# Two layer mixers in another order, with their masks built three heads at a time and 16 chunks' low parts on GpSimd

## The reference

```
proj = h @ w_in                          # 256 x (gate 384, rec 384, z 384, xbc 896, dt 6, uv 512)
rec  = causal_dwconv(rec, 4 taps);  r, i = sigmoid(rec @ w_r + b_r), sigmoid(rec @ w_i + b_i)
a    = exp(-8 r softplus(-lam));    u = sqrt(1 - a*a) * i * rec
ya   = scan(h = a*h + u) * gelu(gate)                        # "recurrent branch", 384 wide
xbc  = silu(causal_dwconv(xbc, 4 taps)); xs, B, C = split(xbc)   # "state-space branch"
dt   = softplus(dt + dt_bias);      ad = dt * -exp(a_log);   cs = cumsum(ad)
yb   = sum_s (C.B)[l,s] * exp(cs[l]-cs[s]) [s<=l] * dt[s] * xs[s] + d_skip * xs   # six heads
yb   = rms_norm(yb * silu(z))
u, v = split(gelu(uv)); v = layer_norm(v); yc = u * (tril(w_s) @ v + b_s)         # "u-v branch"
out  = concat(ya, yb, yc) @ w_out
```

## Time and profile before

| | |
|---|---|
| median of 3 runs | 1672.4 us (1672.17 to 1672.96) |
| profiled execution, its own time | 1670.92 us |
| its span, first to last instruction | 1669.2 us |
| PE busy, share of the span | 94% |
| DVE, ACT, POOL busy | 65%, 48%, 5% |
| mean granted clock of PE | 0.948 of full speed |

### The profile page before, as it was taken

One profiled execution on the slowest core, in us unless ns is written; L12 is line 12 of the kernel. 1 busy time (PEld: TensorE's weight loads), 2 busy tenths in 40 slices (PEclk: granted clock), 3 DMA queues, 4 the chain that ended last, 5 costly groups with the idle time before them and its releaser, 6 DMA issues.

```text
span 1669.2 us, 27509 instructions
## 1 busy us (share of the span) xinstructions
PE 1563.6 (94%) x10201; PEld 1409.1 (84%) x10201; DVE 1083.9 (65%) x1756; ACT 794.6 (48%) x1299; POOL 91.7 (5%) x116
## 2 busy tenths in 40 slices
PE   6999998899999999989799999899888789999999
PEld 5999888789998999979679999698666469989998
DVE  4555686665557655577666555657899966655555
ACT  5333457363335533365644333546476644453332
POOL 0000000000000000010000000103121210000000
PEclk9999998799999999998889999989888779999999
DMA  7555553155555655545135555446111115645552
GB/s 284 189 186 188 187 166 114 61 167 190 187 180 175 230 189 188 181 144 181 38 126 189 187 181 187 134 152 227 64 63 64 38 56 184 194 149 189 186 181 99
DMA packets 71081, 261.88 MB, mean 157 GB/s; under 512 B 8016, under 2 KB 8016, under 8 KB 70736
## 3 DMA queue, kind: packets, MB, share of 16 engines
q1 hardware_dynamic: 69696, 253.79, 46.1%
q10 hardware_dynamic: 1296, 6.85, 1.1%
HBM read 259.56 MB, written 1.05 MB: 156 GB/s over the span
## 4 chain that ended last, share of the span: by engine, by line
PE 77%; DVE 15%; ACT 6%; issue 2%; DMA 1%; POOL 0%; ACTq 0%; DVEq 0%
PE work L437 18%; PE work L439 17%; PE work L438 17%; PE acc L437 7%; PE acc L438 7%; PE acc L439 7%; DVE wlo L432 3%; ACT whi L425 1%; DVE g L1851 1%; DVE rs L1858 1%; DVE sm L1859 1%; DVE xbcc L1099 1%; DVE h L1844 1%; DVE sg L1843 1%; DVE frac L1712 0%
## 5 line engine op out<-in xcount | busy, mean ns | idle before, releaser
L432 DVE TENSOR_TENSOR wlo<-raw,whi 128x1024 fp32r<-128x1024 f32 x480 | 571.5, 1217 | 232.2 <-ACT whi L425 228.6
L437 PE MATMUL work<-xhi,whi 128*128 128x256 f32 x2160 | 616.4, 285 | 7.3 <-DVE wlo L432 5.9
L439 PE MATMUL work<-xhi,wlo 128*128 128x256 f32 x2160 | 613.0, 284 | 0.0
L438 PE MATMUL work<-xlo,whi 128*128 128x256 f32 x2160 | 612.8, 284 | 0.0
L425 ACT ACTIVATE whi<-raw 128x1024 fp32r<-128x1024 f32 x480 | 476.8, 1043 | 28.9 <-PE acc L439 15.9
L437 PEld LDWEIGHTS work<-xhi,whi 128*128 128x128 f32 x2160 | 416.2, 193 | 12.8 <-issue 6.1
L438 PEld LDWEIGHTS work<-xlo,whi 128*128 128x128 f32 x2160 | 416.3, 193 | 4.5
L439 PEld LDWEIGHTS work<-xhi,wlo 128*128 128x128 f32 x2160 | 416.1, 193 | 0.0
L765 ACT ACTIVATE sg<-sg 128x256 f32<-128x256 f32 x100 | 41.9, 419 | 495.9 <-DVE sg L803 495.9
L437 PE MATMUL acc<-whi,hhi 128*128 128x512 f32 x440 | 174.6, 397 | 0.0
L438 PE MATMUL acc<-wlo,hhi 128*128 128x512 f32 x440 | 174.0, 396 | 0.0
(11 more groups left out here) (406 smaller groups left out, 1736.9 us busy)
## 6 DMA issues: line engine op xcount, KB each, us to landing
raw<-stream SPq DMA_DIRECT2D x480, 512.0 KB, 4.2
par<-pm ACTq DMA_DIRECT2D x2, 1644.5 KB, 6.9
pfa<-pf_a ACTq DMA_DIRECT2D x3, 516.0 KB, 3.5
pfb<-pf_b ACTq DMA_DIRECT2D x2, 516.0 KB, 7.9
x<-x_in SPq DMA_DIRECT2D x2, 512.0 KB, 6.3
out<-x SPq DMA_DIRECT2D x2, 512.0 KB, 2.6
par<-pm ACTq DMA_DIRECT2D x1, 820.0 KB, 4.5
pre<-pf_a ACTq DMA_DIRECT2D x1, 4.0 KB, 4.4
```

What stands on the lines that cost most here:

```text
L432: nc.vector.tensor_tensor(chunk(wlo, place, c)[:, cols], chunk(raw, place, c)[:, cols], chunk(whi, place, c)[:, cols].bitcast(F32), ALU.su ...
L437: return [nc.tensor.matmul(o, lhi, rhi, start=start, stop=False), nc.tensor.matmul(o, lhi, rlo, start=False, stop=False), nc.tensor.matmul ...
L438: nc.tensor.matmul(o, lhi, rlo, start=False, stop=False),
L439: nc.tensor.matmul(o, llo, rhi, start=False, stop=stop)]
```

## The change

The order of the mixer's 30 chunks is now: z and dt together in four (`zdt`, 390 columns; the fourth chunk has 48 used columns and only those are split), xbc in seven (B and C first: `XBC_ORDER`), rec in three, gates in three, the padding, u-v in four, `w_out` in eight. PE's program follows, with `cbt` right behind the first rec chunk, the head sums for heads 0 to 2 ahead of the recurrent gates, those of 3 to 5 behind them, all six heads' matmuls behind the gate chunks, u-v behind those, and the mixing `sgu` behind three output chunks. Exponents are kept for three heads together (`dm`, 128x1152), so that ACT does two exponentials and DVE two multiplications (`weights`) instead of six and twelve; dt is multiplied into xs while it is emptied (`xdt`). The low parts of chunks 6 to 21 are made by GpSimd.

```diff
-C_UV, C_REC, C_XBC, C_DT, C_GATE0, C_GATE1, C_Z, C_PAD, C_OUT = 0, 4, 7, 14, 15, 16, 18, 21, 22
-OUT_ORDER = [6, 7, 0, 1, 2, 3, 4, 5]
+C_ZDT, C_XBC, C_REC, C_GATE, C_PAD, C_UV, C_OUT = 0, 4, 11, 14, 17, 18, 22
+ZDT = BW + HEADS
+BY_POOL = range(6, C_OUT)
+XBC_ORDER = [3, 4, 5, 6, 0, 1, 2]
+OUT_ORDER = [0, 1, 2, 3, 4, 5, 6, 7]
+BANKED = (["zdt0", "zdt1"] + [f"xbc{b}" for b in XBC_ORDER] + ["rec0", "cs", "rec1", "rec2", "xtok0", "xtok1", "csb0", "csb1", "csb2"]
+          + [f"lru{b}" for b in range(AB)] + ["csb3", "csb4", "csb5", "gate0", "gate1", "gate2", "uv0", "uv1", "sgu0", "sgu1"]
+          + ["ybt0", "ybt1", "ybt2", "yct0", "yct1"])
+        def split_lo_pool(pool, place, cs):
+            pool.wait_ge(lo_ready, place.count(cs[0] - 1))
+            for c in cs:
+                cols = used(place, c)
+                pool.wait_ge(hi_ready, place.count(c))
+                nc.gpsimd.tensor_tensor(chunk(wlo, place, c)[:, cols], chunk(raw, place, c)[:, cols], chunk(whi, place, c)[:, cols].bitcast(F32),
+                                        ALU.subtract).then_inc(lo_ready, 1)
...
+            for i, b in enumerate(XBC_ORDER):
+                projected(C_XBC + i)
+                emptied(f"xbc{b}", nc.scalar.activation(xbcpad[:, b, 3:], bank(f"xbc{b}", slice(0, S)), ACT.Copy))
+                split_hi(act, place, [C_XBC + i + 6])
+                if i == 5:
+                    activated(range(0, 4))
+            recurrent(0)
+            activated(range(4, 7))
+            recurrent(1)
+            recurrent(2)
+            decays(0)
...
+            def exponents(g):
+                vec.wait(dve, 1)
+                for h in range(3 * g, 3 * g + 3):
+                    job.wait(dve, JOB[f"csb{h}"])
+                    o = dm[:, g, h % 3]
+                    nc.vector.scalar_tensor_tensor(out=o[:, 0:S], in0=bank(f"csb{h}", slice(0, S)), scalar=ncs[:, 0, h:h + 1], in1=maskadd[:, :], op0=ALU.add, op1=ALU.add)
...
+            def weights(g):
+                dexp.wait(dve, g + 1)
+                job.wait(dve, JOB["cbt"])
+                m_ready.inc(nc.vector.tensor_tensor(dm[:, g], dm[:, g], acc[:, 1, g * 512:g * 512 + 384].unsqueeze(1).broadcast_to([P, 3, 384]), ALU.mult))
```

More of the change, by code:

```diff
@@ L885, in release @@
                     m.then_inc(consumed, 1)
-            begin(pe, BANKED, "uv0")
-            done("uv0", tokens("uv0", 0, C_UV, 2 * CW, first=True)[-1])
+            begin(pe, BANKED, "zdt0")
+            done("zdt0", tokens("zdt0", 0, C_ZDT, ZDT, first=True)[-1])
             turn_xn(pe, q, r, 1)
[L890 to L895, removed]
@@ new lines, in mix_pe @@
+            done("cbt", m)
+            begin(pe, BANKED, "cs")
+            ad_ready.wait(pe, 1)
+            tri, ones = upper[:, 0:P], upper[:, P:S]
+            nc.tensor.matmul(bank("cs", slice(0, HEADS)), tri, ad[:, 0, :], start=True, stop=True)
+            nc.tensor.matmul(bank("cs", slice(8, 8 + HEADS)), ones, ad[:, 0, :], start=True, stop=False)
+            done("cs", nc.tensor.matmul(bank("cs", slice(8, 8 + HEADS)), tri, ad[:, 1, :], start=False, stop=True))
+            channels("rec1", C_REC + 1)
@@ new lines, in mix_pe, with sums @@
+            channels("rec2", C_REC + 2)
+            xbc_act.wait(pe, XB)
+            for t in range(T):
+                begin(pe, BANKED, f"xtok{t}")
+                for b in range(AB):
+                    m = nc.tensor.transpose(bank(f"xtok{t}", slice(b * P, (b + 1) * P)), xbcc[:, b, t * P:(t + 1) * P], ident[:, :])
+                done(f"xtok{t}", m)
+            def sums(h):
+                begin(pe, BANKED, f"csb{h}")
+                o = bank(f"csb{h}", slice(0, S))
+                nc.tensor.matmul(o, ad[:, 0, h:h + 1].broadcast_to([P, P]), upper[:, :], start=True, stop=False)
+                done(f"csb{h}", nc.tensor.matmul(o[:, P:S], ad[:, 1, h:h + 1].broadcast_to([P, P]), tri, start=False, stop=True))
@@ L900, in mix_pe @@
+            for h in range(3):
+                sums(h)
             for b in range(AB):
@@ L906, in mix_pe @@
                 done(f"lru{b}", m)
[L907 to L916, removed]
-            begin(pe, BANKED, "cs")
@@ L919, in mix_pe @@
-            ad_ready.wait(pe, 1)
-            tri, ones = upper[:, 0:P], upper[:, P:S]
-            nc.tensor.matmul(bank("cs", slice(0, HEADS)), tri, ad[:, 0, :], start=True, stop=True)
-            nc.tensor.matmul(bank("cs", slice(8, 8 + HEADS)), ones, ad[:, 0, :], start=True, stop=False)
[L923 to L945, removed]
@@ L960, in mix_pe @@
[L960 to L971, removed]
+            for h in range(3, HEADS):
+                sums(h)
@@ new lines, in mix_pe, with gated @@
+            begin(pe, BANKED, "uv0")
+            done("uv0", tokens("uv0", 0, C_UV, 2 * CW)[-1])
+            begin(pe, BANKED, "uv1")
+            release(tokens("uv1", 1, C_UV, 2 * CW), 4)
+            def gated():
+                wst.wait(pe, 1)
+                for t in range(T):
+                    begin(pe, BANKED, f"sgu{t}")
+                    vln.wait(pe, t + 1)
+                    for g in range(4):
+                        m = nc.tensor.matmul(bank(f"sgu{t}", slice(g * HD, (g + 1) * HD)), par[:, PM["w_s"]][:, g * P:(g + 1) * P],
+                                             vx[:, t, g * HD:(g + 1) * HD], start=True, stop=True)
+                    done(f"sgu{t}", m)
@@ L1003, in projected, with recurrent @@
                 act.wait_ge(consumed, place.count(c) + RING)
[L1005 to L1010, removed]
-            for b in range(AB):
+            def recurrent(b):
                 projected(C_REC + b)
@@ L1211, in mix_dve @@
[L1211 to L1215 removed]
+            split_lo(dve, place, range(MIX_CHUNKS, MIX_CHUNKS + 2))
+            vstep.end("vstep")
         def bank2(name, cols=slice(0, 512)):
```

337 lines of the change are left out of this document (171 added, 166 removed).

## The result

The changed kernel takes **1643.5 us** (median of 4 runs, 1642.3 to 1647.0), against 1672.3 of the kernel before in the same session: ratio 0.983, interval 0.9813 to 0.9847. The profiled execution takes 1642.3 itself, its span is 1640.5. The forecast was 1658.5: the direction was right, and the time lies in the range, but the gain of 28.8 us is twice the 13.9 that the sum gave.

A forecast was written before the change was run, and what follows sets the result against it. PE was taken to set the end, working partly at half clock or for too few columns. Savings of 5.2 us in the first mixer and 8.7 in the second make 1672.4 - 13.9 = 1658.5 us; range 1632 to 1678.

The forecast's parts named there:

- the sum: Whole kernel: first mixer ends 5.2 us earlier, second is 8.7 shorter, in all 13.9 us less.
- the dt product: Start of each mixer: 48 small matmuls vanish into z's six extra columns, 6.7 us less and 0.1 more.
- The entry: Before the first mixer: fourth chunk's low part nearly vanishes, `weighted` starts about 0.7 us earlier, first product at 210.7.
- The lock: DVE's SBUF operations and GpSimd's low parts take turns, each for its whole length; PE waits 12.9 and about 7 us.
- The rival that it does not hold for convolutions: Convolutions beside GpSimd run free, or DVE gets several turns for one: 1616 us, chance 0.12.
- half as strong, at 1640: Convolutions beside GpSimd: DVE gets two turns before GpSimd's own, queue shorter than counted; about 1640 us, chance 0.10.
- The step that failed: First mixer, until the fourth block is convolved: GpSimd's and DVE's lengths add up to 257.8, so `cbt` waits 12.9 us.
- Behind the third sum: First mixer from 278.0, through gates, heads, u-v and outputs: 60.7 us, end at 338.7 instead of 343.9.
- The second mixer: Same steps as the first mixer: 127.3 us from 730.1 instead of 136.0, 8.7 less.
- The slower rival: GpSimd's wide low parts take longer: gain lost from 3.1 us each, 1700 us at 4.3; chance 0.16.

The follow-up runs named there:

- e4: The changed kernel with the six dt columns as products of their own again, 48 small matmuls behind those of z; 1660.2 us.
- e2: The kernel before in its own order, with only the low parts of chunks 6 to 21 moved to GpSimd; 1705.3 us.
- e10: The changed kernel with seven extra DVE multiplications on SBUF tiles ahead of the first convolution, beside GpSimd's low parts; one execution, 1646.4 us.
- e1: The changed kernel with all low parts of the mixer's chunks made by DVE again and none by GpSimd; 1621.0 us.

## Why the prediction was right in direction and wrong in size

**What is removed, the dt product: about right.** 6.6 a mixer by the sum, some 8 by e4, of which a part that no run isolates is clock.

**The entry: about right.** `weighted` starts at 206.95 instead of 207.48, and the first product at 210.96, for 210.7 forecast.

**The lock: right as a mechanism.** PE comes to `cbt` at 245.4 (forecast 245.2) and waits there for ACT's Silu behind DVE; DVE's small one-input operations stand in the lock as well. The rival that it does not hold for convolutions is refuted by the 2.5 us of the rows above and by e2; that it is half as strong, at 1640, came near the time, but for another reason: DVE did get one turn for each low part, no more.

**The step that failed** is the term "the lock must carry seven low parts (9 to 15), 17.5 us, four convolutions, 7.6, and five small ones, 0.5: 257.8". It adds the length of each of DVE's operations to GpSimd's. The fourth convolution ended at 254.3, and `cbt` starts at 254.8 instead of 258.1. The row of eight low parts (8 to 15) and what the sum adds to it up to 257.8 splits so:
- The row starts at 229.17 instead of 229.7: 0.5 us.
- A low part alone is 2.35 us instead of 2.5, eight times: 1.2.
- The double count: for what DVE does inside the row, one convolution and the small operations, the sum adds 2.4 us (their free length is 2.8 in the trace), and GpSimd lost 0.7 (19.47 less eight times 2.35): 1.7.

The other three convolutions run free behind the row, 5.7 us, as in the sum. The same two errors, in six convolutions and three low parts, make another 1.6 us between `cbt` and the third sum (18.3 instead of 19.9). The earlier trace rows could have told it: beside low parts of 1.22 us the GpSimd operation of 1.05 lasts 2.05, so it is held for 1.0 and not for the whole 1.22. The prediction took the whole length, and for operations of 0.17 to 0.49 us.

**Behind the third sum** I allowed 60.7 us, and it took 58.4. The 1.3 for gates at half clock were not needed: over gates, heads and u-v the clock is full (window of PE, columns as before):

```profile
280.80:331.50 50.70, 49.90 (x288) 1.00 0.40 127
```

The other 1.0 is what was allowed for latencies; that is by arithmetic, no experiment isolates it. Together, 3.3, 1.6 and 2.3 are the 7.2 by which the first mixer ended early (331.5 for 338.7).

**The second mixer** was to take the same steps, 128.0 us from its first product, and took 122.0; up to `cbt`, to the third sum and behind it, it was 2.6, 1.0 and 2.4 us faster than they. By its end it gained 14.7 instead of 8.7. With the 7.2 of the first mixer, these 6.0 and the 1.6 of the unchanged code behind it, the 14.8 us by which the sum was off are located: 8.5 of them up to the two third sums, where the lock's term stands, 4.7 behind them, 1.6 in unchanged code.

**The slower rival** needed ten low parts a mixer of over 3.1 us. e10 has three at 3.14, and only because DVE's extra operations were of 768 columns; with the wait at `cbt` at 12.6, the loss in the two mixers is 6.4 us. e2 shows what the slower side really needs: an order in which the work that PE wants first lies behind 12 operations in the lock.

**What the change is made of**, from the experiments: the order and the joined dt columns without GpSimd give some 52 us (e1 to before), of them about 16 from the columns (e4, measured beside GpSimd). The move to GpSimd takes 22.5 back. In the old order it would have cost 32.

## What to carry to other kernels

Before moving work from DVE to GpSimd, look at where DVE's inputs lie in the stretch beside it: operations that read PSUM pass freely, operations that read only SBUF get one turn for each of GpSimd's operations, however short they are. So give GpSimd its work where DVE reads PSUM or waits, or leave it on DVE, and put what PE needs last behind what it needs first. In an estimate of two engines that take turns, count turns by the longer partner's length, and add of the shorter one only what it was measured to cost: here nothing for an operation of 0.17 us, 0.24 for one of 0.49, 0.8 for one of 0.95.

## What was not expected of the hardware

A subtraction of 128x1024 with two SBUF inputs takes 2.35 us on GpSimd and 1.22 on DVE. Taking a turn costs DVE up to 2.3 us, and GpSimd nothing for an operation of 3 elements, 0.24 us for one of 256 columns with two inputs and 0.79 for one of 768. Why it is less than the length of DVE's operation was not settled. The Trainium skill ("SBUF — State Buffer", section "SBUF: two separate sides") says that the first to start keeps the port pair for its whole instruction; for DVE, which waits 2.3 of GpSimd's 2.4 us, the traces agree, and for GpSimd they don't: by it turns of 0.49 and 0.95 us would cost as much, and 0.24 and 0.79 were measured, which decides. That an operation with a PSUM input passes fits its wording of two SBUF inputs; that one of three elements with a single SBUF input waits 2.1 us is the earlier trace rows again, 2.32 here for 0.17 when free.
